# Differential attention stage of a three-layer float32 block: VectorE takes one weight split less ahead of its steps from the ninth unit on, and two pairs of turned blocks are made in one visit each

## The reference

```python
q, k, v = split_cols(h @ w_in, [D_MODEL, D_MODEL, D_MODEL])
q = rope(rms_norm(q, g_q), pos)        # 8 heads, two maps of 64 features each
k = rope(rms_norm(k, g_k), pos)
s = einsum('bhtqd,bhtkd->bhtqk', q, k) * scale
pr = softmax(s, axis=-1)
a = pr[:, :, 0] - lam * pr[:, :, 1]
o = rms_norm(einsum('bhqk,bhkd->bhqd', a, v), g_sub) * (1.0 - lambda_init)
return o.reshape(bsz, seq, D_MODEL) @ w_out
```

## Time and profile before

| | |
|---|---|
| median of 3 runs | 906.69 us (906.21 to 907.82) |
| the profiled execution, its own time | 903.17 us |
| its span | 900.7 us, 12220 instructions |
| TensorE matmuls (PE) | 893.2 us busy, 99% |
| VectorE (DVE) | 653.8 us busy, 73% |
| ScalarE (ACT) | 508.2 us busy, 56% |
| GpSimd (POOL) | 53.1 us busy, 6% |
| stream loads | 295 of 512 KB on SyncE's queue, 4.5 us median from issue to landing |

### The profile page before, as it was taken

The page is one execution under the profiler, slowest core; times in us unless marked ns, Lnnn a source line. Parts: engine busy times, 40 slices in busy tenths (PEclk is TensorE's granted clock), DMA queues, the critical chain, the costliest instruction groups (busy, mean ns, idle before and its releaser), DMA issues.

```text
span 900.7 us, 12220 instructions
## 1 busy us (share of the span) xinstructions
PE 893.2 (99%) x4358; PEld 736.1 (82%) x4358; DVE 653.8 (73%) x995; ACT 508.2 (56%) x821; POOL 53.1 (6%) x57
## 2 busy tenths in 40 slices
PE   9999999999999999999999999999999999999998
PEld 8987888888888888778888888888888888877776
DVE  5984478767745689997787777645678898779663
ACT  6755555444444676688664444434665555576691
POOL 0001000000000002211000000000010000212000
PEclk9999999999999999999999999999999999999999
DMA  7574558776765656434387766746667776557611
GB/s 263 202 237 148 159 186 289 279 244 236 245 208 186 219 191 222 151 108 140 129 295 249 248 234 244 249 142 230 198 233 279 257 240 204 204 204 248 208 71 47
DMA packets 81339, 187.53 MB, mean 208 GB/s; under 512 B 10948, under 2 KB 36804, under 8 KB 81288
## 3 DMA queue, kind: packets, MB, share of 16 engines
q1 hardware_dynamic: 80856, 186.20, 60.4%
q10 hardware_dynamic: 432, 0.66, 0.2%
HBM read 171.89 MB, written 14.94 MB: 207 GB/s over the span
## 4 chain that ended last, share of the span: by engine, by line
PE 98%; DVE 0%; DMA 0%; ACT 0%; issue 0%; SPq 0%; ACTq 0%; DVEq 0%
PE bank L1768 87%; PE bank L1795 3%; PE bank L1810 1%; PE bank L2070 1%; PE bank L2096 1%; PE bank L2180 1%; PE bank L2209 1%; PE bank L2081 0%; DMA consts<-consts_dram 0%; PE bank L1917 0%; PE bank L2166 0%; PE bank L2056 0%; PE bank L2190 0%; PE bank L1965 0%; PE bank L1969 0%; DVE wlo L1061 0%
## 5 line engine op out<-in xcount | busy, mean ns | idle before, releaser
L651 ACT ACTIVATE whi<-raw 128x1024 fp32r<-128x1024 f32 x295 | 306.4, 1059 | 186.4 <-DMA raw<-stream_dram 106.9
L1061 DVE TENSOR_TENSOR wlo<-raw,whi 128x1024 fp32r<-128x1024 f32 x296 | 348.7, 1214 | 47.8 <-ACT whi L651 47.3
L1768 PE MATMUL bank<-whi,x_hi 128*128 128x512 f32 x560 | 152.8, 394 | 0.0
L1768 PE MATMUL bank<-wlo,x_hi 128*128 128x512 f32 x560 | 149.9, 389 | 0.0
L1768 PE MATMUL bank<-whi,x_lo 128*128 128x512 f32 x560 | 149.8, 389 | 0.0
L1768 PEld LDWEIGHTS bank<-wlo,x_hi 128*128 128x128 f32 x560 | 105.1, 188 | 22.2
L1768 PEld LDWEIGHTS bank<-whi,x_lo 128*128 128x128 f32 x560 | 105.1, 188 | 22.0
L1768 PEld LDWEIGHTS bank<-whi,x_hi 128*128 128x128 f32 x560 | 103.3, 188 | 22.0 <-issue 1.7
L1768 PE MATMUL bank<-whi,y_hi 128*128 128x512 f32 x400 | 109.5, 394 | 0.0
L1768 PE MATMUL bank<-wlo,y_hi 128*128 128x512 f32 x400 | 107.5, 389 | 0.0
L1768 PE MATMUL bank<-whi,y_lo 128*128 128x512 f32 x400 | 107.5, 389 | 0.0
(11 more groups left out here) (239 smaller groups left out, 870.7 us busy)
## 6 DMA issues: line engine op xcount, KB each, us to landing
raw<-stream_dram SPq DMA_DIRECT2D x295, 512.0 KB, 4.5
ffn_blocks<-ffn_blk SPq DMA_DIRECT2D x22, 256.0 KB, 2.0
ffn_land<-ffn_blocks SPq DMA_DIRECT2D x22, 256.0 KB, 3.8
second_blocks<-h_blk SPq DMA_DIRECT2D x8, 256.0 KB, 2.0
h_land<-second_blocks SPq DMA_DIRECT2D x8, 256.0 KB, 2.8
cv_blocks<-cv_blk SPq DMA_DIRECT2D x7, 256.0 KB, 4.0
cv_land<-cv_blocks SPq DMA_DIRECT2D x7, 256.0 KB, 3.4
h_blocks<-h_blk SPq DMA_DIRECT2D x3, 512.0 KB, 6.0
```

What stands on the lines that cost most here:

```text
L651: A(whi[:, u % RING, :], raw[:, u % RAW, :], ACT.Copy).then_inc(sem("w_hi"), 1)
L1061: V.tensor_tensor(wlo[:, u % RING, :], raw[:, u % RAW, :], whi[:, u % RING, :].bitcast(F32), ALU.subtract).then_inc(sem("w_lo"), 1)
L1768: last = T.matmul(bank[pair + t][:, :], lhs[a][:, kt, t * P:(t + 1) * P], w[:, u % RING, kk * NW:(kk + 1) * NW], start=part != 1 and k == ...
```

## The change

Three things differ. VectorE's steps at unit 9 of the stage and later are preceded by splits up to u+4 and no longer u+5. TensorE makes block 1 at unit 8 with block 0 (before: at unit 11), and block 5 at unit 18 with block 4 (before: block 4 at 17, block 5 at 19); at unit 18 the order is then blocks 4 and 5, scores of head 3, aT 1, where aT 1 came ahead of the scores. ScalarE copies block 1 at its step 10 (before: 12) and block 5 at 17, ahead of the copy of aT 1 (before: at 18, behind it and behind the exponentials of head 3).

```diff
 DF_ORDER = {
     "pe": (
-        (1, "second", 0), (8, "qkT", 0), (11, "qkT", 1), (12, "qkT", 2), (13, "scores", 0), (13, "qkT", 3),
-        (13, "scores", 1), (16, "scores", 2), (16, "aT", 0), (17, "qkT", 4), (18, "aT", 1), (18, "scores", 3),
-        (19, "qkT", 5), (20, "qkT", 6), (20, "qkT", 7), (20, "scores", 4), (20, "aT", 2), (21, "scores", 5),
+        (1, "second", 0), (8, "qkT", 0), (8, "qkT", 1), (12, "qkT", 2), (13, "scores", 0), (13, "qkT", 3),
+        (13, "scores", 1), (16, "scores", 2), (16, "aT", 0), (18, "qkT", 4), (18, "qkT", 5), (18, "scores", 3),
+        (18, "aT", 1), (20, "qkT", 6), (20, "qkT", 7), (20, "scores", 4), (20, "aT", 2), (21, "scores", 5),
...
     "act": (
-        (4, "tile", 0), (8, "tile", 1), (9, "qkT", 0), (12, "qkT", 1), (12, "tile", 2), (12, "qkT", 2),
+        (4, "tile", 0), (8, "tile", 1), (9, "qkT", 0), (10, "qkT", 1), (12, "tile", 2), (12, "qkT", 2),
         (13, "qkT", 3), (14, "scores", 0), (15, "scores", 1), (16, "tile", 3), (16, "aT", 0), (16, "scores", 2),
-        (17, "qkT", 4), (17, "aT", 1), (18, "scores", 3), (18, "qkT", 5), (19, "qkT", 6), (19, "qkT", 7),
+        (17, "qkT", 4), (17, "qkT", 5), (17, "aT", 1), (18, "scores", 3), (19, "qkT", 6), (19, "qkT", 7),
...
             for u, step, arg in df_order("dve"):
-                split_to(u + AHEAD)
+                split_to(u + AHEAD - (1 if u >= END[DF_IN] + 9 else 0))
```

## The result

The changed kernel is slower: 915.39 us median of 5 runs against 906.21, ratio 1.0098 with a 95% interval of 1.0087 to 1.0109, that is 8.9 us (7.9 to 9.9); the two medians by themselves differ by 9.2. Slower was right, the size was not: 911.9 was forecast, and 914.6 was the end of the range.

A forecast was written before the change was run, and what follows sets the result against it. TensorE, busy 893.2 of 900.7 us, was taken to bound the kernel. Late loads gave a net +5.2 us, the 0.6 of savings included, on the median of 906.69: 911.9, range 909.2 to 914.6.

The forecast's parts named there:

- the mechanism and its places: Attention stage: late wlo splits delay raw loads, ScalarE stands still before whi splits, TensorE waits for ScalarE; +5.2 us.
- Block 2 and the merged visit: TensorE: 0.54 us wait before block 2 goes, merging blocks saves some 0.05; -0.6 us in all.
- Waits on whi 20 and whi 22: ScalarE: waits for raw grow from 9.1 us by some 10, one of 5 or more, one near 2.5.
- The first chain: From split 15 behind unit 1, through late raw 20 and raw 22, to aT 1: unit 18's wlo group +5.67 us.
- the sum: Step-by-step times along the late loads, wlo 16 done at 373.48; +5.2 us with savings inside, 908.4 for the profiled execution.
- twice the median 3.3: Bound on the two raw transfers: +0.4 us, where 3.10 us each was taken from a lone load.
- Behind this I find no more.: After aT 1: no further loss; blocks 6 and 7 in time, ScalarE up to 0.2 us later at whi 26, whi 30.
- The first, no chain and -0.6: Raw 20 lands early enough that ScalarE does not wait; only the savings remain, -0.6 us, 906.1; chance 0.07.
- The second, the first link only: Exponentials of heads 0 and 1 hold TensorE, raw 22 does not hold ScalarE; +2 to +2.4 us, 909; chance 0.08.
- the third: More than the sum: TensorE's clock falls to 1.2 GHz for one or two units, +2.7 to +5.4 us; chance 0.08.
- further late link worth over 1.5 us: A later late step (block 6, or a slow transfer) adding over 1.5 us; chance 0.07.

The follow-up runs named there:

- act_less: The whole change, with ScalarE's splits also one less ahead from its step 14 on; ratio 0.9995 (0.9985 to 1.0006) against the kernel before.
- best: The kernel before with only blocks 0 and 1 merged and VectorE one split less ahead at step 10 alone; ratio 1.0000 (0.9991 to 1.0009).
- first_link: The kernel before with VectorE one split less ahead at its steps 10 and 11 only; ratio 1.0047 (1.0029 to 1.0065).

## Why the prediction was wrong

**Right: the mechanism and its places.** Block 2 and the merged visit: -0.6, measured -0.62. Waits on whi 20 and whi 22, VectorE idle before soft 0 (3.8 us said, 4.06 measured), TensorE's waits before the scores of head 2, unit 16, block 5 and aT 1 (2.5 said, 2.42 measured). act_less shows the cause. ScalarE's waits for raw grew by 15.4 us, not by some 10.

**The first chain was mis-sized.** It was given +5.67 at unit 18's wlo group, which began at 397.92; less the 1.66 of the start and against 389.49 that is +6.77. Of the 1.1 us, 0.36 was there when wlo 16 ended (375.50, or 373.84 on the old scale, for the 373.48 of the sum). I had let tile 2's squares begin with TensorE's end of unit 11; they began 0.24 later, behind whi 18, which waited for raw 18 until 365.49. The other part is the landings, for which I took 3.10 us from one load. SyncE's timeline of the changed kernel:

```profile
375.67 0.33 SPq L454 DMA_DIRECT2D raw<-stream_dram  x1
...
384.94 0.33 SPq L454 DMA_DIRECT2D raw<-stream_dram  x1
385.93 0.34 SPq L441 DMA_DIRECT2D raw<-stream_dram  x1
```

The first two are the issues of raw 20 and raw 22; whi 20 began 3.34 us and whi 22 3.47 us later, 0.6 above the sum together, and some 0.1 was added in handing over. The prediction had both loads alone on the queue, and they were not: raw 21 was issued at 378.40, 0.6 us before whi 20 began, and raw 23 at 385.93. Its bound of twice the median 3.3 covered most of this; the value taken was near the lowest.

**The step that failed is "Behind this I find no more."** I looked at whi 26 and whi 30 and gave ScalarE 0.2 us of delay there. The tail lost 2.56 us: 0.87 between units 22 and 24, 1.56 between units 25 and 26, 0.13 later. Raw 32 needs wlo 28, which had moved behind VectorE's step of the first pair, the sums and a soft, and I had not asked for it. VectorE's rows, first before, then in the changed kernel; the wlo is split 28 in both:

```profile
414.58 1.22 DVE L1061 TENSOR_TENSOR wlo<-raw,whi 128x1024 fp32r<-128x1024 f32 x1
416.32 0.88 DVE L1077 SCALAR_TENSOR_TENSOR x_lo<-bank,cols,x_hi 128x256 fp32r<-128x256 f32 x2 [0.53 <-ACT x_hi L662]
```

```profile
425.51 0.88 DVE L1077 SCALAR_TENSOR_TENSOR x_lo<-bank,cols,x_hi 128x256 fp32r<-128x256 f32 x2 [1.78 <-ACT x_hi L662]
...
429.12 1.22 DVE L1061 TENSOR_TENSOR wlo<-raw,whi 128x1024 fp32r<-128x1024 f32 x1
```

So whi 32 waited 2.52 us, ahead of the step that frees bank 7 for pair 1, and TensorE waited 1.24. For raw 30 I had the place but not the size: TensorE waited 0.62 us before unit 24. Raw 30 needs wlo 26, and ahead of that now stand wlo 24 and 25 and the maxima of head 6. The 5.2 us forecast, the 1.1 of the first chain and these 2.56 are 8.86, against the 8.85 measured at unit 30.

**Rivals.** The first, no chain and -0.6, could not have happened as priced: best has no chain and gains nothing, because unit 16 was already timed by head 1's exponentials. The sum names that claim for the late case and forgets it for the early one. The second, the first link only, had its price too low: +2 to +2.4 against 4.07 in first_link, which keeps the old visits (the price had some 0.4 for the merged ones). Unit 16 was 3.27 us late there and not 2.4, and soft 1, late for aT 1, was left out. Of the third, the lower clock did not come. In the stretch with the wait of 2.42 us the granted clock stayed at 1.00, 2.4 GHz (busy time of PE, PEld, DVE, ACT, POOL; clock, DMA share, GB/s):

```profile
390.00:400.00 10.00, 6.79 (x40) 5.21 (x39) 9.68 (x22) 9.19 (x23) 3.36 (x2) 1.00 0.28 89
```

The "further late link worth over 1.5 us" of the same rival is what happened, at the 0.07 I gave it: two links, 2.4 us.

## What to carry to other kernels

Where a buffer ring ties a load to work on one engine and another engine must take that load in program order, a step is paid for by what is queued behind the next load, not by when the consumer needs the data: here one wlo, done 16 us before TensorE took it, cost 4 us when it was done 8 us later. When the look-ahead of one engine in such a ring is cut, cut that of the engine that takes the loads as well, so that its steps don't stand behind them. And follow a change that holds for a whole loop to the last iteration; ask of an idle time that is to be removed what the next wait behind it is, before counting it as a gain.

## What was unexpected of the hardware

TensorE stood still for 2.42 us in one piece with no change of the granted clock (1.00 from 390 to 400 us). Loads of 512 KB on a nearly empty queue took 3.10, 3.34 and 3.47 us from issue to use (whi 21 before, whi 20 and 22 after), so a chain of two carries some 0.6 us that one row does not show.
